# One streaming step of a hybrid encoder layer on one core: the convolution's projections as 36 units between the parts of both attentions

## What is computed

```python
proj = rmsnorm(x, g_mix) @ w_in          # 1024 -> 3600 columns
dn_qkv, dn_z, dn_alpha, dn_beta, sb_q, sb_k, sb_v = split(proj)
c = silu(causal_conv(dn_qkv, conv_w, conv_state))   # 4 taps, 1536 channels
q, k, v = split(c)                        # DeltaNet heads, 8 x 64
o_a = gated_delta_rule(l2norm(q) / 8, l2norm(k), v, g, beta, s0)   # chunks, one state
o_a = rmsnorm(o_a, g_out_dn) * silu(dn_z)
# stick-breaking attention, 8 heads x 64; the sample also sees 2048 cached rows
z = q_b @ k_b.T / 8
a = sigmoid(z) * reversed_cumulative_product(1 - sigmoid(z))   # later keys, strictly causal
o_b = a @ v_b
h = x + concat(o_a, o_b) @ w_out
h = h + square(relu(rmsnorm(h, g_mlp) @ w_up)) @ w_down
h = h + sigmoid(rmsnorm(h, g_ple) @ w_ple_gate) * (p @ w_ple_proj)
```

## Time and profile before

| | |
|---|---|
| time, median of 3 runs | 2078.79 us (2076.92 to 2079.15) |
| the profiled execution: its time, its span | 2082.88 us, 2081.0 us |
| PE busy | 1873.1 us, 90% of the span |
| DVE, ACT, POOL busy | 808.4, 489.0, 611.9 us |
| matmuls | 15913 |
| moved by the DMA engines | 104.62 MB, 50 GB/s on the mean |

### The profile page before, as it was taken

How to read it: one execution, slowest core, us unless ns; L and a number is a source line. 1 busy time by engine, 2 the same in 40 slices (tenths; PEclk the granted TensorE clock), 3 DMA queues, 4 the chain that set the end, 5 groups by cost and what they waited for, 6 DMA issues and landing times.

```text
span 2081.0 us, 36339 instructions
## 1 busy us (share of the span) xinstructions
PE 1873.1 (90%) x15913; PEld 1728.6 (83%) x15913; DVE 808.4 (39%) x938; ACT 489.0 (23%) x854; POOL 611.9 (29%) x267
## 2 busy tenths in 40 slices
PE   4989999967775599989889999999999999997899
PEld 4989989945553378878779999999999999997767
DVE  5551225548783265656412521221212121217222
ACT  4221132246564222322121301010101001014110
POOL 4133314500000654443104424343333424343000
PEclk9999999979998698999789999999999999999999
DMA  4121312120004201011021111111111111111200
GB/s 158 42 70 55 111 39 89 42 72 1 1 1 147 91 18 43 22 28 26 21 79 41 41 41 61 34 47 47 54 40 40 40 40 60 40 40 50 71 28 37
DMA packets 90897, 104.62 MB, mean 50 GB/s; under 512 B 9493, under 2 KB 74337, under 8 KB 90785
## 3 DMA queue, kind: packets, MB, share of 16 engines
q1 hardware_dynamic: 81440, 89.96, 13.6%
q10 hardware_dynamic: 9344, 12.98, 1.7%
HBM read 85.32 MB, written 17.60 MB: 49 GB/s over the span
## 4 chain that ended last, share of the span: by engine, by line
PE 83%; DVE 5%; ACT 4%; DMA 2%; issue 2%; POOL 2%; SPq 0%; ACTq 0%; DVEq 0%; POOLq 0%
PE psum L1573 47%; PE psum L1545 5%; PE psum L1546 5%; PE psum L1547 5%; PE psum L1861 2%; PE psum L1866 2%; PE psum L1619 2%; PE psum L1645 2%; PE psum L1849 2%; PE psum L1633 1%; ACT area L943 1%; PE psum L1622 1%; PE psum L1744 1%; DVE area L1193 1%; PE psum L1801 1%
## 5 line engine op out<-in xcount | busy, mean ns | idle before, releaser
L656 POOL TENSOR_TENSOR w_hi<-w_raw,ones 128x2048 fp32r<-128x2048 f32 x51 | 185.0, 3628 | 1068.9 <-PE psum L1573 620.8
L1573 PE MATMUL psum<-act_hi,w_hi 128*128 128x352 f32 x1248 | 270.0, 324 | 0.8 <-ACT area L1072 0.8
L1573 PE MATMUL psum<-act_hi,w_lo 128*128 128x352 f32 x1248 | 268.9, 323 | 0.0
L1573 PE MATMUL psum<-act_lo,w_hi 128*128 128x352 f32 x1248 | 268.6, 323 | 0.0
L657 POOL TENSOR_TENSOR w_lo<-w_raw,w_hi 128x2048 fp32r<-128x2048 f32 x51 | 254.8, 4996 | 4.0
L1545 PE MATMUL psum<-w_hi,act_hi 128*128 128x256 f32 (+1 forms) x720 | 226.3, 314 | 28.3 <-issue 17.2
L1546 PE MATMUL psum<-w_lo,act_hi 128*128 128x256 f32 (+1 forms) x720 | 222.0, 308 | 0.0
L1547 PE MATMUL psum<-w_hi,act_lo 128*128 128x256 f32 (+1 forms) x720 | 220.9, 307 | 0.0
L1573 PEld LDWEIGHTS psum<-act_hi,w_lo 128*128 128x128 f32 x1248 | 214.2, 188 | 0.0
L1427 DVE TENSOR_TENSOR area<-psum,area 128x1056 f32<-128x1056 f32 x72 | 90.5, 1257 | 317.3 <-PE psum L1573 317.3
L1573 PEld LDWEIGHTS psum<-act_hi,w_hi 128*128 128x128 f32 x1248 | 212.4, 189 | 0.9 <-ACT area L1072 0.9
(11 more groups left out here) (266 smaller groups left out, 2622.5 us busy)
## 6 DMA issues: line engine op xcount, KB each, us to landing
w_raw<-in_w_up_dram SPq DMA_DIRECT2D x16, 1024.0 KB, 5.6
w_raw<-in_w_down_dram SPq DMA_DIRECT2D x16, 1024.0 KB, 5.0
w_raw<-in_w_in_dram SPq DMA_DIRECT2D x14, 1024.0 KB, 5.5
area<-in_x_prompt_dram SPq DMA_DIRECT2D x16, 512.0 KB, 4.1
conv_scratch<-area ACTq DMA_DIRECT2D x12, 512.0 KB, 2.7
area<-conv_scratch SPq DMA_DIRECT2D x8, 768.0 KB, 4.8
w_raw<-in_cache_k_dram SPq DMA_DIRECT2D x2, 2048.0 KB, 9.1
area<-in_cache_v_dram SPq DMA_DIRECT2D x2, 2048.0 KB, 8.7
```

The costliest lines, as they stand in the source:

```text
L656: own.link(pool.tensor_tensor(hi, w_raw[:, slot, :], ones[:, 0:1].to_broadcast([P, BLK]), ALU.mult))
L1573: last = pe.matmul(bank(base + c)[0:rows, 0:CH], w(k), a[:, k, CH * c:CH * (c + 1)], start=(k == 0 and w is lhs_hi and a is hi), stop=(k = ...
```

## The change

The projections of the convolution leave their stage. Each of the twelve tiles becomes three units of 352 columns, all in bank 7; unit f is tile f // 3, columns 352 (f % 3) on, 24 matmuls. PE issues units 0 and 1 behind the first two `scores`, one behind the weights of each step (none in steps 8, 16 and 24), one behind the last `values` (number SU = 31) and four between the parts of the stream's attention. Per unit ACT places it in `xb`, with the three columns before it, and writes the last tap into `yb` (in the third part of a tile DVE makes that tap too); DVE adds the other taps; ACT makes a sigmoid into `conv_gate`, POOL multiplies it in, and SP stores `yb` (one transfer, two for the third part). So Silu is made as y * sigmoid(y).

The weights of the convolution come as twelve half blocks, two of them in slot 0, split by POOL between its gates; slot 1 and the room of its low part receive the cached keys. The units read `act_hi` and `act_lo` until the last one, so a step's output can no longer be split into them: ACT copies it from bank 6 to `o_st`, SP stores it in `o_dram`, and after the stream's attention SP loads all outputs into `w_raw`, ACT copies them into `act_hi` and DVE subtracts into `act_lo`. The first two blocks of `w_out` are loaded after that and are split by POOL inside its DeltaNet loop, after chunks 4 and 5; the other two blocks are loaded late in the DeltaNet. The tails are turned after the stream. In the stream, `stream_scores(1)` stands behind the end of the first group. Block numbers and semaphore counts follow.

The diff, cut to its core:

```diff
+    o_dram = nc.dram_tensor("o_scratch", (WT, P, TP), F32).ap()
+        UNIT_OF = {-2: 0, -1: 1}
+        for s in range(len(STEPS)):
+            if s % 8 or s == 0:
+                UNIT_OF[s] = len(UNIT_OF)
+        SU = len(UNIT_OF)
 # SP
+            def store_unit(f):
+                m, c = f // 3, f % 3
+                sp.wait_ge(cs_ready, f + 1)
+                n = CH if c < 2 else TP - 2 * CH
+                sp.dma_start(conv_dram[m, :, CH * c:CH * c + n], yb[:, f % 2, 0:n]).then_inc(cs_stored[f % 2], 16)
+                if c == 2:
+                    sp.dma_start(conv_dram[m, :, TP:T], yb[:, f % 2, n + 3:CY]).then_inc(cs_stored[f % 2], 16)
+                if f % 3 == 1 and 4 <= (f + 11) // 3 < NC:
+                    conv_weights_in((f + 11) // 3)
+            def store_heads(step):
+                i, t = STEPS[step]
+                sp.wait_ge(o_kept, step + 1)
+                sp.dma_start(o_dram[i, :, P * t:P * (t + 1)], o_st[:, step % 2, :]).then_inc(o_moved[step % 2], 16)
+            for step in range(len(STEPS)):
+                if unit_of(step - 3) is not None:
+                    store_unit(unit_of(step - 3))
+                if step >= 2:
+                    store_heads(step - 2)
...
             conv_in(0, P)
             z_in(0, P)
+            for u in range(2):
+                block_in(20 + u, u, wout[:, :, 256 * u:256 * u + 256], before=(o_split, 2 * u + 2))
...
             z_in(NT, TS)
+            for u in range(2):
+                block_in(22 + u, u, wout[:, :, 512 + 256 * u:768 + 256 * u])
 # POOL
+            def gate_unit(f):
+                n = CH if f % 3 < 2 else CY
+                pool.wait_ge(conv_sig, f + 1)
+                pool.tensor_tensor(yb[:, f % 2, 0:n], yb[:, f % 2, 0:n], conv_gate[:, 0:n],
+                                   ALU.mult).then_inc(cs_ready, 1)
-            for u in range(2):
-                split(8, u, dense_ready, NC - 2 + 2 * u)
+            for f in range(UNITS):
+                gate_unit(f)
+                if f % 3 == 1 and 2 <= (f + 5) // 3 < NC:
+                    split_conv((f + 5) // 3)
             pool.wait_ge(so_split, 2)
...
                     decay_logs(c + 3, P if c + 3 < NT else TS)
+                if c == NT - 4:
+                    split(12, 0, unit_ready, UNITS)
+                elif c == NT - 3:
...
+                    split(12, 1, tails_stored, 32)
 # ACT
+            def place_unit(f):
+                m, c = f // 3, f % 3
+                x, y, src = xb[:, f % 2, :], yb[:, f % 2, :], bank(7)
+                act.wait_ge(unit_ready, f + 1)
+                if f >= 2:
+                    act.wait_ge(y_ready, f - 1)
+                    act.wait_ge(cs_stored[f % 2], cs_count(f - 2))
...
+                    own.mark(act.activation(x[:, 3:3 + CH], src[:, 0:CH], ACT.Copy))
+                    act.activation(y[:, 0:CH], src[:, 0:CH], ACT.Copy, scale=taps[:, 3, m:m + 1]).then_inc(xb_ready, 1)
...
+            def unit_sigmoid(f):
+                n = CH if f % 3 < 2 else CY
+                act.wait_ge(y_ready, f + 1)
+                if f:
+                    act.wait_ge(cs_ready, f)
+                act.activation(conv_gate[:, 0:n], yb[:, f % 2, 0:n], ACT.Sigmoid).then_inc(conv_sig, 1)
             for step in range(len(STEPS)):
+                if step:
+                    keep_heads(step - 1)
                 for u in range(2):
                     copy_weights(step, u)
                     if step + 2 < len(STEPS):
                         sigmoids(step + 2, u)
+                if unit_of(step) is not None:
+                    place_unit(unit_of(step))
+                    unit_sigmoid(unit_of(step) - 1)
...
+            for i in range(WT):
+                act.wait_ge(raw_loaded[i // 2], 16 * 11)
+                act.activation(act_hi[:, WT + i, 0:TP], heads_raw[i // 2][:, i % 2, :], ACT.Copy).then_inc(o_high, 1)
 # DVE
+            def convolve(f):
+                m, n = f // 3, CH if f % 3 < 2 else CY
+                x, y = xb[:, f % 2, :], yb[:, f % 2, 0:n]
+                dve.wait_ge(xb_ready, f + 1)
+                if f % 3 == 2:
+                    own.link(dve.tensor_scalar(y, x[:, 3:3 + n], taps[:, 3, m:m + 1], None, ALU.mult))
+                for tap in range(3):
+                    last = dve.scalar_tensor_tensor(out=y, in0=x[:, tap:tap + n], scalar=taps[:, tap, m:m + 1], in1=y,
+                                                    op0=ALU.mult, op1=ALU.add)
...
-                if step >= 2:
-                    split_out(step - 2)
+                if unit_of(step - 2) is not None:
+                    convolve(unit_of(step - 2))
...
+            for i in range(WT):
+                dve.wait_ge(o_high, i + 1)
+                dve.tensor_tensor(act_lo[:, WT + i, 0:TP], heads_raw[i // 2][:, i % 2, :],
+                                  act_hi[:, WT + i, 0:TP].bitcast(F32), ALU.subtract).then_inc(o_split, 1)
 # PE
+            def conv_unit(f):
+                m, c = f // 3, f % 3
+                if c == 0:
+                    pe.wait_ge(w_split, 8 + m + 1)
+                if f:
+                    pe.wait_ge(xb_ready, f)
...
-            scores(0)
-            scores(1)
+            for step in range(2):
+                scores(step)
+                conv_unit(step)
             for step in range(len(STEPS)):
                 if step:
                     values(step - 1)
...
                 turn_weights(step, 1)
+                if unit_of(step) is not None:
+                    conv_unit(unit_of(step))
             values(len(STEPS) - 1)
+            conv_unit(SU)
...
             turn_cache(0)
             stream_scores(0)
+            conv_unit(SU + 1)
             turn_cache(1)
+            conv_unit(SU + 2)
...
-                    elif g == 0:
-                        stream_scores(1)
...
+                if g == 0:
+                    stream_scores(1)
+                    conv_unit(SU + 3)
+                    conv_unit(SU + 4)
```

367 lines of the change are left out of this document (208 added, 159 removed).

## The result

The changed kernel took 2025.62 us (median; 2012.22 to 2026.49) beside 2078.97 for the kernel before on the same chip: a ratio of 0.973, 95% interval 0.9697 to 0.9764, 53 us less. The forecast was 2031, 48 less. The profiled execution took 2025.65 and its span is 57.3 shorter.

The account below looks back on a forecast made before the run. PE was taken to bound the kernel, with standing time to fill. From 287.5 to 685.1, 397.6 us becomes 278 + 12 + 59 = 349; entry -7.1, splits +8: -47.7 from 2078.8, so 2031 us, range 1998 to 2062.

Parts of the forecast that it names:

- Where the time is: Both attentions and the stretches beside them: 92 us of standing PE, latencies between engines that other PE work can fill.
- PE from 287.5: Attention with units: PE's attention work 143.8 us plus 124.5 for 32 units of 3.89 us each.
- the pair that was to cancel: Attention: switching tile shapes costs 5 us, a higher clock gives back about as much (143.8 x 0.04).
- The start: Begin of the attention: scores(1) waits for step 0's sigmoids, which ACT begins late; 6 us.
- The waits that stay: Attention: the three steps without a unit keep PE's wait for ACT, 1.34 us each, 4 in all.
- The locks of DVE and POOL: Attention: POOL's splits and gates and DVE's SBUF work exclude each other; 12 us, bounds 0 and 26.
- The sum of 254 us: Attention: DVE 130 plus 54 and POOL 70 us, one after the other, fitting under PE's 278.
- SP: "Nothing, unless POOL is late": SP's single order of stores and weight loads in the attention costs nothing; a store lands in 2.7 us.
- rival 3's ring: Attention: ACT's `place_unit` waits through gate and store, 11.5 us a step; +19, about 2098 us; chance 0.08.
- The stream: The stream's attention grows by 7.6 us, from 51.4 to 59, bounds 52 and 66.
- The entry: Entry to the DeltaNet: PE starts after 3.4 us instead of 10.5, -7.1; bounds -8 to -3.
- The splits in the loop: DeltaNet loop: two w_out splits on POOL hold DVE's decayed queries, 4 us each, +8; bounds 0 and 14.

Follow-up runs that it names:

- the lower group: The faster executions of the changed kernel, run once more unaltered: 2010.07 and 2010.09 us.
- the upper group: The slower executions of the changed kernel, run once more unaltered: 2023.19, 2023.27, 2023.78 and 2026.99 us.

## Why the prediction was right, and where it was not

**Where the time is** was right. PE's standing time in both attentions was latency, the units fill it, and PE's wait before `values` fell from 42.8 to 2.4 us. Matmuls of a unit came out as costed: the next PE instruction starts 4.0 us after the first matmul at the full clock, against 3.89 and 0.17 for the switch of shapes. No table is loaded between steps, as forecast.

**PE from 287.5** was sized 7 us too long: 268.3 forecast, 261.13 busy. The step that failed is the pair that was to cancel, the clock (0.04 x 143.8 = 5.8 less) and the switches (5 more). By the single records of the trace (a matmul's end is modelled) the attention's own matmuls are busy 136.1 instead of 143.8, 7.7 less, as the stage's clock rose from 0.92 to 0.96; the 32 units, busy 135.0 by themselves, add only 125.0 to that, because for 10.0 us the end of one matmul lies over the start of the other kind. So the switches added 0.5 to the 124.5, not 5. Without splits and stall the stage had 0.99, and PE was busy 256.0, 12.3 under the forecast.

**The start** (6 forecast, 6.3 measured) was right. **The waits that stay** were in part: the three steps without a unit keep 0.81 each, 2.4 instead of 4, and four waits before `turn_weights` (3.7) were not in the sum.

**The locks of DVE and POOL**, 12 us, are the term that was mis-sized: at most 5.5 by the kernel without splits. The sum of 254 us that it was weighed with was fair (DVE was busy 240, and 257 is where the stage stands with PE's work cut). Wrong was where the splits fall: five of ten on wide steps at 2 to 3 us each was the reckoning, and no split met a scan of 896 or 1024 columns; most held taps, and of these holds PE felt little. The sign named beforehand, scans longer than 2.29, came (2379 on average) but stood for something else: one scan of eight, which took 3.03 us behind a gate. The rule from the Trainium skill (SBUF — State Buffer, Who interferes with whom), that a DVE instruction with two inputs in SBUF contends with a POOL instruction that reads SBUF, agrees with that scan.

**SP: "Nothing, unless POOL is late"** was wrong, and hid the first error: 9.7 us of standing and 2.4 with the clock. The step looked at who waits in SP's order and took 2.7 us for every store. It did not go through what SP issues just ahead of each store at the end of the steps, a load of 2 MB, behind which 176 KB landed in 8.1 us. It is rival 3's ring, at one place; and the sign named beforehand, ACT's largest wait a unit's store, was there (13.06, ACT's longest single wait of that stage).

**So the attention's stage** was near its forecast in part by luck (283.3 against 290): the store's 9.7 stand where the sum had 12 for the locks.

**The stream** came to 54.5 against 59 (bounds 52 and 66), near the end at which all units are hidden. **The entry** was right: 2.9 against 3.4, and the kernel before with the splits moved (3.06) shows POOL's order as the cause.

**The splits in the loop** were right in mechanism and place, decayed queries behind POOL's two instructions, and under-sized: 4 each forecast, bounds 0 and 14 together, 12.4 measured in the two chunks (41.8 + 43.2 against 37.0 + 35.7), and 17.5 in all by the kernel that moves them, with what the low clock behind them cost. The pricing by one value was the mistake: who comes first decides between two, and 12 to 13 us hang on it.

**Up to the convolution** nothing was forecast and 4.6 came, 2.8 of it traced: the new half blocks of weights hold DVE, and through it ACT and PE, for less. The prediction had this lock in its hands and applied it only where the change adds POOL work, not where it shortens what POOL already did.

The six misses (-4.6, -6.7, -4.5, -0.5, +5.8, +0.9) come to -9.6; without their signs they are 23.0. So the total was closer than its parts by luck, and luck too is which group the median fell into: with more executions in the lower group it would have been 13 us less.

Still open: what puts the queries ahead of the split in some executions of the same kernel, what lowers the clock in an early chunk of some executions, and what causes the long low stretch of the clock at the loop's end.

## What to carry to other kernels

Where work fills another engine's gaps, price each queue it passes by what is issued right ahead of it: a small store that gates a buffer goes ahead of a large load, not behind. Where POOL and DVE both work on SBUF, put a long POOL instruction behind the DVE instruction that the bound engine needs next, and cut it in pieces; here order was worth 20 us (against the upper group) and pieces 12 to 16, without removing any work. When two engines come within a few per cent of each other in a stage, take work from one to see where the other stands before filling further.

## What the runs showed of the hardware

- Which of the two comes first decides who is held: a query 0.21 us ahead of a split made the split 4.05 us instead of 3.60, a query 1.33 us behind it grew, as a pair, from 1.41 to 7.72. The Trainium skill (SBUF — State Buffer, Who interferes with whom) says that "Issue order, not op shape, decides who blocks"; these rows agree.
- The hold lasts for the POOL instruction that runs, then one DVE instruction gets in: in the changed kernel the first query took 2.81 us, to 0.54 behind the end of the split's first instruction, and the second 4.89, to 0.55 behind the end of its second; with halves of 1024 columns the pairs took 3.87 and 4.62 us.
- The prediction reckoned with this only for DVE instructions that read SBUF twice. The first tap of a unit's third part, a product with one tensor as input (L1363), took 1157 ns on average in the changed kernel and 455 without the splits.
- A transfer of 176 KB issued 0.43 us behind one of 2 MB on the same queue landed after 8.1 us; ahead of it such stores took 2.0.
